# Second kind of mixer: head means by one block constant, one mask per stick head, and logits and output sums placed elsewhere

## The reference, cut to what matters

```python
qa = apply_partial_rope(rmsnorm_2(heads(qa, 4), qk_g[layer, 0]), cos, sin)   # likewise ka, qb, kb
oa = moba_attention(qa, ka, heads(va, 4))
ob = dsa_attention(qb, kb, heads(vb, 4), qi, ki, wi)
oc = stick_breaking_attention(heads(qc, 8), heads(kc, 8), heads(vc, 8))
o = jnp.concatenate([oa, ob, oc], axis=2)
o = _rms(o).reshape(B, S, D_MIX) * out_g[layer]      # one mean square per head of 64
x = x + g2 * (o @ w_out[layer])

# stick_breaking_attention, for one block of 128 queries:
z = einsum('bqhd,bshd->bhqs', qb, k) * scale
strict = kpos[None, :] < t[:, None]
log_beta = log_sigmoid(z)
log_1m = where(strict, log_sigmoid(-z), 0.0)
after = cumsum(log_1m, axis=3, reverse=True) - log_1m
a = where(strict, exp(log_beta + after), 0.0)
o = einsum('bhqs,bshd->bqhd', a, v)
```

## Time and profile before

| | us |
|---|---|
| median of 3 runs (lowest, highest) | 2524.24 (2522.84, 2525.45) |
| the profiled execution: time, span | 2521.16, 2519.1 |
| PE busy in the span | 2486.2 |
| DVE, ACT, POOL busy | 2079.9, 1577.4, 206.2 |
| mean granted TensorE clock | 0.997 of full speed |

### The profile page before, as it was taken

One profiled execution on the slowest core, in us unless ns is written; L12 is line 12 of the kernel. 1 busy time (PEld: TensorE's weight loads), 2 busy tenths in 40 slices (PEclk: granted clock), 3 DMA queues, 4 the chain that ended last, 5 costly groups with the idle time before them and its releaser, 6 DMA issues.

```text
span 2519.1 us, 44296 instructions
## 1 busy us (share of the span) xinstructions
PE 2486.2 (99%) x17300; PEld 2260.6 (90%) x17300; DVE 2079.9 (83%) x2845; ACT 1577.4 (63%) x2325; POOL 206.2 (8%) x275
## 2 busy tenths in 40 slices
PE   9999999999999999999999999999999999999999
PEld 9999998999999999999998899987899899987998
DVE  5789857999999999999998899775888898775665
ACT  5644566888888888888886644555544544555543
POOL 2111021000000000000000111013011010013000
PEclk9999999999999999999999999999999999999999
DMA  7698546999999999999998687423687687431542
GB/s 295 236 360 317 195 152 236 388 366 375 370 377 371 373 371 374 371 368 377 370 389 333 242 312 299 152 108 118 251 310 291 231 320 268 151 126 51 212 181 76
DMA packets 136637, 696.54 MB, mean 277 GB/s; under 512 B 16528, under 2 KB 16656, under 8 KB 87728
## 3 DMA queue, kind: packets, MB, share of 16 engines
q1 hardware_dynamic: 109872, 599.12, 63.7%
q0 software_dynamic: 23424, 88.16, 9.1%
q10 hardware_dynamic: 3136, 6.43, 0.7%
HBM read 683.61 MB, written 13.24 MB: 277 GB/s over the span
## 4 chain that ended last, share of the span: by engine, by line
PE 91%; DVE 5%; ACT 2%; issue 1%; POOL 1%; DVEq 0%; ACTq 0%; POOLq 0%
PE ps L2398 16%; PE ps L1963 15%; PE ps L1964 15%; PE ps L1965 15%; PE ps L2560 12%; PE ps L2400 8%; DVE w_parts L1687 1%; PE ps L1991 1%; PE ps L2530 1%; DVE w_parts L1332 1%; PE ps L1987 1%; DVE a_parts L1695 1%; PE ps L2292 1%; ACT w_parts L1118 1%; PE ps L2324 0%
## 5 line engine op out<-in xcount | busy, mean ns | idle before, releaser
L2398 PE MATMUL ps<-a_parts,w_parts 128*128 128x512 f32 x1760 | 618.7, 394 | 0.4
L1687 DVE TENSOR_TENSOR w_parts<-ring,w_parts 128x1024 fp32r<-128x1024 f32 x448 | 548.6, 1225 | 52.9 <-ACT w_parts L1118 51.4
L1963 PE MATMUL ps<-w_parts 128*112 128x256 f32 x1792 | 516.0, 288 | 0.0
L1965 PE MATMUL ps<-w_parts 128*112 128x256 f32 x1792 | 499.1, 279 | 0.0
L1964 PE MATMUL ps<-w_parts 128*112 128x256 f32 x1792 | 498.9, 278 | 0.0
L2400 PE MATMUL ps<-a_parts,w_parts 128*128 128x256 f32 x1760 | 493.2, 280 | 0.0
L1118 ACT ACTIVATE w_parts<-ring 128x1024 fp32r<-128x1024 f32 x448 | 471.9, 1054 | 0.0
L2398 PEld LDWEIGHTS ps<-a_parts,w_parts 128*128 128x128 f32 x1760 | 330.1, 188 | 73.4 <-issue 3.2
L2400 PEld LDWEIGHTS ps<-a_parts,w_parts 128*128 128x128 f32 x1760 | 333.3, 189 | 0.0
L1963 PEld LDWEIGHTS ps<-w_parts 128*112 128x112 f32 x1792 | 313.7, 175 | 11.7 <-issue 0.2
L1964 PEld LDWEIGHTS ps<-w_parts 128*112 128x112 f32 x1792 | 313.4, 175 | 11.7
(11 more groups left out here) (275 smaller groups left out, 4535.2 us busy)
## 6 DMA issues: line engine op xcount, KB each, us to landing
ring<-wstream SPq DMA_DIRECT2D x378, 1024.0 KB, 7.2
ring<-wstream SPq DMA_DIRECT2D x378, 512.0 KB, 5.9
proj<-astream POOLq DMA_DIRECT2D x144, 512.0 KB, 5.6
slot_rows<-branch POOLq DMA_DIRECT2D x7, 448.0 KB, 6.9
slot_out<-slot_rows POOLq DMA_DIRECT2D x1, 3136.0 KB, 15.5
sq<-slot_rows ACTq DMA_DIRECT2D x49, 64.0 KB, 5.3
slot_out<-pT ACTq DMA_DIRECT2D x49, 64.0 KB, 5.4
cst<-consts SPq DMA_DIRECT2D x1, 1692.0 KB, 14.1
```

What stands on the lines that cost most here:

```text
L1687: nc.vector.tensor_tensor(up_lo[:, n % 2, at], ring[:, s, at], up_hi[:, n % 2, at], ALU.subtract)\
L1963: mm(o, stationary[0], moving[0], start=start, stop=False, skip_group_check=True)
L1965: return mm(o, stationary[1], moving[0], start=False, stop=stop, skip_group_check=True)
L2398: mm(ps[:, bank, :], hi, a_parts[:, :, k, :], start=k == 0, stop=k == KB - 1, skip_group_check=True)
```

## The change

Selector and spreading constants go; in their place stands one constant `headmean` of 128 x 128 with 1/64 within a head and 0 elsewhere. A product with it gives each channel its head's mean square, on all 128 partitions. A constant `barred` holds 0 where the strict mask allows and 1e30 elsewhere; POOL adds it to the second term of each stick head before the exponential, in place of the multiply after it. `logits` 1 and 2 are issued one place earlier, and the sums of the output blocks are six (`o_sum` 0 to 5: two blocks each for 0 and 1, one each for 2 to 5), all in PSUM bank 6, each waiting for the root of the one before. The roots are now taken on 128 partitions and written to SBUF, over the squares.

```diff
-for _n, _w in (("ident", P), ("headsel", KB * 16), ("spread", KB * P), ("rot", P), ("after", P),
+for _n, _w in (("ident", P), ("headmean", P), ("rot", P), ("after", P),
...
+    put("headmean", np.where(i[:, None] // HD == i[None, :] // HD, 1.0 / HD, 0.0))
+    put("barred", np.where(strict, 0.0, -NEG))
...
 POOL, sticks(m)
-                for h in range(10):
-                    if h < 8:
-                        pool.wait_ge(sp_ready, n + h + 1)
-                        tensor_tensor(st_d[:, h % 4, 0, :], st_d[:, h % 4, 0, :], C("strict"), ALU.mult)  # spm_ready
-                    if h > 1:
-                        g = h - 2
-                        pool.wait_ge(a_exp, n + g + 1)
-                        tensor_tensor(st_a[g % 4], st_a[g % 4], C("strict"), ALU.mult)                    # a_ready
+                for h in range(8):
+                    pool.wait_ge(sp_ready, n + h + 1)
+                    tensor_tensor(st_d[:, h % 4, 0, :], st_d[:, h % 4, 0, :], C("strict"), ALU.mult)      # spm_ready
+                    tensor_tensor(st_d[:, h % 4, 1, :], st_d[:, h % 4, 1, :], C("barred"), ALU.add)       # barred_ready
...
 ACT, key_root(m)
-                inverse_root(norm_s[0:16, 1, :], norm_s[0:16, 0, :], SS[0:16, 0:T], ...)
+                for g in range(2):
+                    dst = hT[:, 4 * g:4 * g + 4, :]
+                    act.wait_ge(qss_ready, 2 * (m - 2) + g + 1)
+                    inverse_root(dst, dst, ps[:, 4 + 2 * g:6 + 2 * g, :]..., V("eps")).then_inc(root_ready, 1)
...
+            def o_root(m, j):
+                dst = o_root_of(j)
+                act.wait_ge(o_sums, 6 * (m - 2) + j + 1)
+                inverse_root(dst, dst, ps[:, 6, 0:dst.shape[1] * T]..., V("eps")).then_inc(o_rooted, 1)
...
 ACT, mixer2(m)
                 copy_out(u + 2, 2)
                 log_term(m, 0)
+                log_term(m, 1)
                 in_copies(m, 26, 27)
                 copy_turned(u + 3)
-                log_term(m, 1)
+                log_term(m, 2)
                 copy_out(u + 3, 2)
-                log_term(m, 2)
...
                 stick_exp(m, 2)
-                first_root(m)
+                o_root(m, 0)
                 log_term(m, 5)
                 stick_exp(m, 3)
+                o_root(m, 1)
...
                 stick_exp(m, 7)
                 cat_hi(m, range(2, 4))
+                o_root(m, 2)
+                copy_sticks(m, 2)
                 hi_half(out, 1, 1)
-                copy_sticks(m, 2)
                 copy_sticks(m, 3)
-                cat_norm(m)
+                for j in range(3, 6):
+                    o_root(m, j)
+                    cat_hi(m, [j + 1])
+                cat_hi(m, [7])
+                hi_outproj(out)
...
 DVE, qk_scaled and cat_scaled: the factor now comes from SBUF
-                                                       ps[:, 4 + b // 2 % 2, (b % 2) * T:(b % 2 + 1) * T],
+                                                       hT[:, b, :], ALU.mult, ALU.mult).then_inc(qk_ready, 1)
...
-                    by = ps[:, cat_bank(p), (k % 2) * T:(k % 2 + 1) * T]
+                    j = k // 2 if k < 4 else k - 2
+                    by = o_root_of(j)[:, k % 2 if k < 4 else 0, :]
...
                 exponent(5)
+                cat_scaled(m, 2)
+                cat_scaled(m, 3)
                 softplus(7)
                 exponent(6)
-                cat_scaled(m, 2)
-                cat_scaled(m, 3)
                 exponent(7)
-                for k in range(2):
+                for k in range(4):
                     cat_rest(m, k)
                 lo_outproj(m, 1, 0)
-                for k in range(2, 4):
-                    cat_rest(m, k)
+                cat_scaled(m, 4)
                 lo_outproj(m, 1, 1)
-                cat_norm(m)
+                cat_rest(m, 4)
+                for k in range(5, KB):
+                    cat_scaled(m, k)
+                    cat_rest(m, k)
...
 PE, mixer2(m) after the change
+                tails(m, 0); values(u + 3, ...); logits(m, 3); tails(m, 1); logits(m, 4); tails(m, 2)
+                weigh(m, 0); o_sum(m, 0); logits(m, 5); tails(m, 3); weigh(m, 1); o_sum(m, 1)
+                logits(m, 6); tails(m, 4); weigh(m, 2); logits(m, 7); tails(m, 5); weigh(m, 3)
+                tails(m, 6); weigh(m, 4); tails(m, 7); weigh(m, 5); o_sum(m, 2)
+                weigh(m, 6); o_sum(m, 3); weigh(m, 7)
 PE, outproj1(m)
                     blocks(0, 0)
+                    o_sum(m, 4)
                     blocks(0, 1)
-                    cat_sums(m, 1)
                     blocks(0, 2)
+                    o_sum(m, 5)
                     blocks(0, 3)
-                    blocks(1, 0)
-                    blocks(1, 1)
-                    cat_spread(m, 2)
-                    cat_spread(m, 3)
-                    for p in range(2, CAT_FIRST):
+                    for p in range(CAT_FIRST):
                         blocks(1, p)
```

More of the change, by code:

```diff
@@ L347, in build @@
         a_exp = sem("a_exp")
[L348 removed]
+        barred_ready = sem("barred_ready")
         co_ready = sem("co_ready")
@@ L877, in copy_out @@
                 if u >= 8:
-                    nc.scalar.activation(o_sq[b // 2][:, :, tt * P:(tt + 1) * P], o, ACT.Square, scale=HD ** -0.5)\
+                    nc.scalar.activation(o_sq[b // 2][:, :, tt * P:(tt + 1) * P], o, ACT.Square)\
                         .then_inc(o_squares, 1)
@@ L1004, in copy_sticks @@
                 o = ps[:, weigh_bank(pair), 0:T]
-                nc.scalar.activation(sq[:, 4 + pair, :], o, ACT.Square, scale=HD ** -0.5).then_inc(co_squares, 1)
+                nc.scalar.activation(sq[:, 4 + pair, :], o, ACT.Square).then_inc(co_squares, 1)
                 nc.scalar.activation(cat[:, 4 + pair, :], o, ACT.Copy).then_inc(co_copied, 1)
@@ L2084, in between_units @@
                     pe.wait_ge(ir_ready, 16 * (l + 1))
-                    head_sums(qss_ready, SS, [(b, hT[:, b, :]) for b in range(KB)])
+                    for b in range(KB):
+                        ins = mm(ps[:, 4 + b // 2, (b % 2) * T:(b % 2 + 1) * T], C("headmean"), hT[:, b, :],
+                                 start=True, stop=True)
+                        if b % 4 == 3:
+                            ins.then_inc(qss_ready, 1)
                 for j in ROPE_JOBS.get(n, ()):
+                    if j == 3:
+                        pe.wait_ge(root_ready, 2 * (l + 1))
                     b, w = PAIRS[j]
@@ L2260, in column_sums, with o_sum @@
                 return ins
[L2262 removed]
+            def o_sum(m, j):
                 l = m - 2
[L2265 removed]
+                if j == 0:
                     pe.wait_ge(pt_copied, 4 * m + 4)
[L2267 to L2283 removed]
+                else:
+                    pe.wait_ge(o_rooted, 6 * l + j)
+                if j < 2:
+                    pe.wait_ge(o_squares, 4 * l + 2 * j + 2)
+                else:
+                    pe.wait_ge(co_squares, 4 * l + j - 1)
+                squares = o_root_of(j)
+                for b in range(squares.shape[1]):
+                    ins = mm(ps[:, 6, b * T:(b + 1) * T], C("headmean"), squares[:, b, :], start=True, stop=True)
+                ins.then_inc(o_sums, 1)
             def mixer1(m, n):
@@ L2287, in mixer1 @@
                 outproj1(m)
-            def head_sums(ready, o, squares):
-                for i, (b, sq_b) in enumerate(squares):
-                    ins = mm(o[0:16, 0:T], C("headsel")[:, b * 16:(b + 1) * 16], sq_b,
-                             start=i == 0, stop=i == len(squares) - 1)
-                ins.then_inc(ready, 1)
             def logits(m, h):
@@ L2372, in mixer2 @@
                 weigh(m, 5)
+                o_sum(m, 2)
                 weigh(m, 6)
+                o_sum(m, 3)
                 weigh(m, 7)
@@ L2700, in _constants @@
     put("ident", np.eye(P))
-    sel = np.zeros((P, KB, 16))
-    for b in range(KB):
-        sel[i, b, 2 * b + i // HD] = 1.0
-    put("headsel", sel)
-    spread = np.zeros((P, KB, P))
-    spread[0:16] = sel.transpose(2, 1, 0)
-    put("spread", spread)
+    put("headmean", np.where(i[:, None] // HD == i[None, :] // HD, 1.0 / HD, 0.0))
     rot = np.zeros((P, P))
```

102 lines of the change are left out of this document (34 added, 68 removed).

## The result

The changed kernel takes 2499.6 us (2498.7 to 2500.0) against 2523.5 (2521.6 to 2525.5): ratio 0.9907, 95% interval 0.9895 to 0.9918, 23.9 us faster. 2505.5 was forecast. Two further sets of executions gave 2499.0 and 2499.5. The profiled execution has a span of 2497.7 and took 2499.8.

The account below looks back on a forecast made before the run. TensorE was taken as the bound. Per mixer -4.0 us (first half) and -3.9 (second), -15.8 for both, plus -3.0 for the clock: -18.8, giving 2502.4 from the profiled execution, 2505.5 us as median; range 2498 to 2511.

Parts of the forecast that it names:

- What bounds the kernel: Whole kernel: TensorE bounds it, busy 2486 of 2519 us; a product removed from its list saves its full duration unless a wait replaces it.
- First half, -4.0: Scaling of q and k, per mixer: spreads removed 3.84 us and changes between product kinds 0.2, wider sums at 0.
- changes between kinds of product: On PE, a product after a foreign one takes 0.44 instead of 0.34 us; 0.2 saved was booked in each half.
- Second half, -3.9: Stick heads and output, per mixer: -7.8 us removed, +2.7 new waits, +1.2 for DVE and POOL excluding each other.
- the exclusion: DVE scalings of blocks 2 and 3 with two SBUF operands and POOL block each other, making `tails(7)` 1.2 us later.
- The wait of 2.28 at `weigh(7)`: Last stick head: PE's 2.28 us wait for POOL's second mask was counted as removed.
- Clock, -3.0: Both mixers: two of three low-clock stretches, 1.5 us each, go with the spreads; ends 0 and -4.5.
- The first: Rival, both mixers: DVE and POOL don't meet and no low stretch is left, -22.7 us, 2501.5; chance 0.17.
- The second: Rival, both mixers: the low clock stays or moves to the new waits, 2508.5 us; chance 0.15.
- the first half gives nothing: Rival, q and k scaling: ACT's wide roots run late and PE waits at the scores, 2513.5 us; chance 0.06.
- POOL doesn't set the pace: Denies the rival in the stick heads: POOL's two operations per head set the pace, +8.6 us a mixer, 2541; chance 0.03.
- What would show it: Signs after: no spreads, unit 17 at about 1651.3, DVE's waits gone, short PE waits, tile 2's split at about 1740.

## Why the prediction was right, and where it was off

The forecast was -18.8 us from the profiled execution; the kernel gained 23.9 from median to median. Summed from the start of each product on PE to the start of the next, one mixer divides so (us; the dividing line is the start of unit 25, waits of PE stand by themselves, and the 1.5 us of the low stretch are taken off the split products of before):

| | before | after |
|---|---|---|
| **first half**: spreads | 3.84 | 0 |
| sums | 3.56 | 3.27 |
| rotations | 2.82 | 2.33 |
| split products | 30.29 | 30.47 |
| the rest, a wait of 0.93 in it | 7.92 | 7.92 |
| **second half**: spreads | 4.27 | 0 |
| waits | 3.59 | 2.81 |
| sums | 3.66 | 3.98 |
| split products | 19.69 | 19.83 |
| the rest | 23.66 | 23.69 |

By the steps of the prediction:

- **What bounds the kernel** holds. What leaves PE's list without a new wait comes back in full: both halves, the added narrow products (+2.1 expected, +2.1 measured) and the shortened waits (1.8 for 1.8). Two readings were wrong, though. PE does wait in the first half, 0.93 us at a transposition, in both kernels alike; and it waits before the last head, too:
```profile
1702.67 1.15 PE L2239 MATMUL ps<-pT,vtok 128*64 128x128 f32 x16 [0.25 <-ACT pT L898]
```
  This 0.25 at `values` is gone in the kernel after, and no term of the sum has it.
- **First half, -4.0**: 4.4 measured. Spreads removed 3.84 as said. The term that was mis-sized is the changes between kinds of product, 0.2 in the forecast: by the table they are 0.6 (0.29 at the sums, 0.49 at the rotations, less 0.18 at the split products). The head means were bounded as 0 to +0.9 on the argument that less is out, and came out cheaper by that 0.29. ACT's roots, 4.3 forecast to end half a us early, took 4.30 from 1648.00 and ended 0.30 early. DVE's waits of 2.27 and 2.22 went.
- **Second half, -3.9**: 9.0 - 4.4 = 4.6. `tails(7)` was given 0.85 and 1.2 for the exclusion, 2.05, and waits 1.65; of this 0.84 is the exclusion. `tails(6)` 0.16 against 0.15. `o_sum(3)` and `o_sum(4)` wait 0.41 and 0.52 where 0.85 each was said. New waits 2.8 instead of 3.9, and 0.25 more of old waits gone than booked. Of these 1.3 only 0.7 shows, because the changes between kinds, booked as -0.2, are +0.5: the sums, now six groups instead of two, cost 0.32 more and the split products 0.14.
- **The wait of 2.28 at `weigh(7)`** was booked as gone with the second mask. It is gone, but not for that reason: with the mask back on POOL nothing changes, and in the kernel before the order of DVE's subtractions alone takes 1.6 of it. The last 0.7 has gone with the rest of the new order, in which the mask ends 1 us early. The size was right by luck, the cause was wrong; the row with the 2.58 us mask lying over the 1.74 us subtraction had shown it, and I used it only for the exclusion elsewhere.
- **Clock, -3.0**: the step that failed. All low stretches in the mixers went, not two of three. From the profiled execution (three of them, and none in the mixture of experts) the gain is 21.4 us, and the parts give 18.1 + 3 x 1.5 - 0.85 for the low stretch that the profile after has there = 21.7. The other 2.6 us of the 23.9 are nearly all the baseline, which is itself a matter of the clock: another execution of the kernel before, at 2523.1 close to the median, has four in the mixers, and with these 18.1 + 4 x 1.5 = 24.1. That four or more is usual rests on this one profile and on the times: of the 27 executions of the kernel before in the later sets 22 took 2522.2 or more, where the one with three took 2521.2. (The mean granted clock can't tell them apart: both profiles have 0.997.) I had seen one execution. It was 3 us under the median, the forecast even says so, but added this back as a constant of the method. With 0.9 for the first half, 1.4 for the second and 3.0 for the clock the miss of 5.1 is accounted for, to 0.2.
- **Rivals.** The first (2501.5: no low clock left, DVE and POOL don't meet) names the half that happened, no low clock; they do meet. The second was thought less likely because no low stretch followed the wait of 2.28 in the first mixer; in the other profile one does. That the low clock stays, that the first half gives nothing and that nothing shows are refuted by the profile and by undoing the first half. POOL doesn't set the pace: 0.99 to 1.18 for each operation.
- **What would show it**: unit 17 early, the split at 1740 (1740.35, and that closely by luck: this execution reached the sums 1.5 us later than the kernel before did and then took 1.1 us less than was forecast), short waits at `tails(7)`, `o_sum(3)` and `(4)`, POOL disturbed about head 6 only: all seen.

The Trainium skill (SBUF — State Buffer, "Who interferes with whom") has it that a VectorE instruction with two SBUF inputs contends with a GpSimd one that reads SBUF, and one with at most one SBUF input, outside the 2-port modes, doesn't. The traces agree, and both sides are now measured here: 1.73 and 1.18 us with two SBUF operands, 0.87 and 1.00 with one in PSUM, the order being the same.

**Open:** what brings the low clock. The places say something. In the three profiles with the kernel before's spreads at the output (its own two and the one with DVE's order changed) a low stretch lies at or behind the last spreads in every one of the six mixers. Behind `weigh(7)` one lies in two of the four mixers where it waits 2.28 us, and in neither of the two where it waits 0.70. None lies in any mixer of the eleven other profiles. Narrow products don't bring it, added alone; the q and k spreads don't; waits of 1.65, 0.5 and 0.4 us don't. What the first place has and no variant has by itself is the 1.06 us wait at the last spreads with the four of them around it, which I didn't try. That this brings the low clock isn't shown.

## What to carry to other kernels

Where two engines exclude each other, look for the pair in the rows and ask which of the two stands ahead of the critical one: the same collision cost 0.84 us ahead of `softplus(7)` and almost nothing behind `exponent(6)`, and moving one long subtraction in the kernel before gave 7 us where the whole change gave 24 (3.2 by the wait, the rest probably by the clock). Undo each part of a change before crediting it: the part that looked responsible for the largest wait was worth nothing. And book a change between kinds of product at each place where one is added, too: here they were the term that was off in both halves. Take a profile of the kernel before twice: stretches of low clock differ from one execution to the next, and a span below the median may mean that some are missing from it.

## What the runs showed of the hardware

- Two scalings of 128x256 took 0.87 us with one operand in PSUM and 1.73 to 1.79 when both were in SBUF and POOL was at work on SBUF (0.87 when it wasn't). With GpSimd's 128x384 mask first, its time stayed 1.00 and a pair of VectorE subtractions of 128x256 on SBUF took 1.35 instead of 0.77.
- Eight fp32 products of 256 columns took 3.47 to 3.56 us, with 16 or 128 output columns, added up in one place or each by itself. What a group costs also depends on what follows: the split product behind started 0.35 or 0.07 us before its recorded end.
- A stretch of 3.41 us at the lower of the two clock levels (1.2 GHz) cost 1.5 us in a mixer, and about 0.85 in the mixture of experts, from the comparison of two profiles. In the same kernel the mixers had three of them in one execution and four in another, of about 2520 us.
